# Attention values on 64 columns: neighbouring key tiles in two column halves, gathered in phases

## The reference, cut to what matters

```python
s_c = einsum(qg, k_cmp);  p_c = masked_softmax(s_c, ...)      # 63 compressed blocks
o_c = einsum(p_c, v_cmp)
imp = einsum(p_c, overlap); idx = top_k(imp + forced, 8)      # 8 of 16 blocks of 64 keys
o_s = einsum(softmax over the selected keys, v_s)             # selected branch
o_w = einsum(softmax over the last 512 keys, v_w)             # window branch
o = g[0] * o_c + g[1] * o_s + g[2] * o_w
```

## Time and profile before

| | us |
|---|---|
| median of three runs | 3420.3 |
| the profiled execution | 3416.0 |
| its span in the trace | 3414.2 |
| attention, first value matmul to last output | about 615 |
| TensorE busy in the span | 3256.0 (95%) |
| VectorE busy | 1531.2 (45%) |
| ScalarE busy | 1229.9 (36%) |
| GpSimd busy | 289.7 (8%) |

### The profile page before, as it was taken

The page is one execution under the profiler, slowest core; times in us unless marked ns, Lnnn a source line. Parts: engine busy times, 40 slices in busy tenths (PEclk is TensorE's granted clock), DMA queues, the critical chain, the costliest instruction groups (busy, mean ns, idle before and its releaser), DMA issues.

```text
span 3414.2 us, 40195 instructions
## 1 busy us (share of the span) xinstructions
PE 3256.0 (95%) x15510; PEld 2674.1 (78%) x15510; DVE 1531.2 (45%) x2409; ACT 1229.9 (36%) x1919; POOL 289.7 (8%) x503
## 2 busy tenths in 40 slices
PE   7999987899999999999999999999978999999997
PEld 5888876788888887888888778667766788888886
DVE  6552456655553344543543542575545322323233
ACT  3641146666666123321321231375513321212121
POOL 0110013333323100000000000110000000000000
PEclk9999989999999999999999999999988999999999
DMA  3222310000000511111111131000101111111111
GB/s 131 81 77 72 117 62 1 1 1 1 1 1 1 186 60 43 49 49 49 49 49 44 49 122 50 25 1 24 40 19 50 62 50 49 49 49 44 48 50 68
DMA packets 48110, 168.35 MB, mean 49 GB/s; under 512 B 6784, under 2 KB 7936, under 8 KB 47600
## 3 DMA queue, kind: packets, MB, share of 16 engines
q1 hardware_dynamic: 37008, 126.49, 11.9%
q0 software_dynamic: 10976, 40.15, 3.3%
HBM read 144.07 MB, written 16.78 MB: 47 GB/s over the span
## 4 chain that ended last, share of the span: by engine, by line
PE 90%; DVE 5%; ACT 3%; issue 1%; DMA 0%; POOL 0%; SPq 0%; DVEq 0%; ACTq 0%
PE PS L223 66%; PE PS L802 6%; PE PS L243 2%; PE PS L793 2%; PE PS L1467 2%; PE PS L778 2%; PE PS L1443 2%; PE PS L777 2%; PE PS L1456 1%; PE PS L820 1%; PE PS L812 1%; DVE SST L1807 0%; PE PS L297 0%; DVE SST L1803 0%; ACT QS L573 0%
## 5 line engine op out<-in xcount | busy, mean ns | idle before, releaser
L201 DVE TENSOR_TENSOR WLO<-RAW,WHI 128x1024 fp32r<-128x1024 f32 x220 | 269.4, 1224 | 1020.5 <-ACT WHI L196 1020.1
L196 ACT CAST WHI<-RAW 128x1024 fp32r<-128x1024 f32 x220 | 231.4, 1052 | 1368.0 <-PE PS L223 1348.5
L223 PE MATMUL PS<-HLO,WHI 128*128 128x512 f32 x2176 | 671.1, 390 | 0.0
L223 PEld LDWEIGHTS PS<-HLO,WHI 128*128 128x128 f32 x2176 | 409.0, 188 | 85.5
L223 PE MATMUL PS<-X_HI,WHI 128*128 128x512 f32 x1520 | 470.5, 391 | 4.5 <-DVE W L318 2.2
L223 PE MATMUL PS<-X_HI,WLO 128*128 128x512 f32 x1520 | 468.0, 389 | 0.0
L223 PEld LDWEIGHTS PS<-X_HI,WHI 128*128 128x128 f32 x1520 | 284.2, 188 | 66.8 <-DVE W L318 2.7
L223 PEld LDWEIGHTS PS<-X_HI,WLO 128*128 128x128 f32 x1520 | 285.5, 188 | 59.5
L223 PE MATMUL PS<-HID_HI,WHI 128*128 128x512 f32 x864 | 267.0, 390 | 5.0 <-DVE HID_LO L1187 5.0
L223 PE MATMUL PS<-HID_HI,WLO 128*128 128x512 f32 x864 | 266.5, 390 | 0.0
L223 PE MATMUL PS<-HID_LO,WHI 128*128 128x512 f32 x864 | 266.5, 390 | 0.0
(11 more groups left out here) (308 smaller groups left out, 4772.0 us busy)
## 6 DMA issues: line engine op xcount, KB each, us to landing
RAW<-in_w SPq DMA_DIRECT2D x220, 512.0 KB, 3.6
X<-in_x SPq DMA_DIRECT2D x8, 512.0 KB, 8.0
Q<-QN POOLq DMA_DIRECT2D x32, 128.0 KB, 2.7
merged<-W POOLq DMA_DIRECT2D x8, 512.0 KB, 3.3
gate<-W POOLq DMA_DIRECT2D x8, 512.0 KB, 2.9
W<-gate POOLq DMA_DIRECT2D x8, 512.0 KB, 4.0
W<-merged POOLq DMA_DIRECT2D x8, 512.0 KB, 4.7
X<-in_x POOLq DMA_DIRECT2D x8, 512.0 KB, 10.9
```

The lines of the kernel that those rows point to most:

```text
L196: nc.scalar.copy(WHI[:, slot, :], RAW[:, slot, :]).then_inc(w_hi, 1)
L201: nc.vector.tensor_tensor(WLO[:, slot, :], RAW[:, slot, :], WHI[:, slot, :].bitcast(F32), ALU.subtract).then_inc(w_lo, 1)
L223: last = nc.tensor.matmul(o[:, half], w[:, slot, cols], x(k)[:, half], start=(k == 0 and w is WHI and x is hi), stop=(k == kcs - 1 and w i ...
```

## The change

The value matmuls take only the 64 columns of V of the pair's own group. The first tile of a chunk writes partitions 0 to 63 of `O_PS`, the second, and the compressed branch, partitions 64 to 127; the output's start partition places each in one column half of the array. The two halves are two partial sums: a new `dve_out_sum` copies the first from PSUM into `O_SUM` and adds the second, and then frees `O_PS`. `act_out_hi` and `dve_out_lo` read `O_SUM`, and a new semaphore `o_lo` stands where `o_free` stood at the end. The uses are gathered: a pair's chunks form one batch (up to four chunks) or two (the first has half of them, rounded up), and all matmuls of a batch stand together in TensorE's queue. The last batch of a pair is used in the next pair's iteration, behind the transposes of its first batch; the odd head's scores stand behind that. `PT` has eight buffers. `act_out_hi` stands behind copy 2 (or the last) instead of copy 0. `O_SUM` lies where `POOL_W` lay.

```diff
--- before.py
+++ after.py
@@ -133,6 +133,7 @@
     QK_W = fix("QK_W", [4])
     QS_W = fix("QS_W", [1])
     GATE = fix("GATE", [QT, N_GATE])
+    POOL_W_AT = at
     POOL_W = fix("POOL_W", [N_POOL, P])
     POOL_INV = fix("POOL_INV", [N_POOL, 16])
     POOL_SC = fix("POOL_SC", [N_POOL])
@@ -674,7 +675,8 @@
     MSEL = [sb(f"MSEL{i}", [T], X_AT + 8 * KB + 4 * KB * i) for i in range(2)]
     P_LONG = [sb(f"P_LONG{i}", [T + 5 * P], H_AT + 6656 * i) for i in range(4)]
     P_SHORT = [sb(f"P_SHORT{i}", [T], H_AT + 4 * KB * i) for i in range(6)]
-    PT = [sb(f"PT{i}", [4, P], W_AT + 12 * KB + 2 * KB * i) for i in range(4)]
+    PT = [sb(f"PT{i}", [4, P], (W_AT + 12 * KB if i < 4 else R + 24 * KB) + 2 * KB * i) for i in range(8)]
+    O_SUM = [sb(f"O_SUM{i}", [2, P], POOL_W_AT + KB * i) for i in range(2)]
     O_HI = sb("O_HI", [HPG, T], R, F32R)
     EC = sb("EC", [HPG, HEAD], W_AT)
     PCG = sb("PCG", [HPG, HEAD], W_AT + 2 * KB)
@@ -688,9 +690,9 @@
     T_PS = [PS[:, 2 * T + 512 * i:2 * T + 512 * i + 512] for i in range(2)]
     O_PS = [PS[:, 3 * T + 512 * i:3 * T + 512 * i + 2 * P] for i in range(2)]
     C0_PS = PS[:, 3 * T + 512:4 * T]
-    s_done, shifted, exp_done, inv_done, p_done, t_done, pt_copied, pv_done, o_hi, o_free = (
+    s_done, shifted, exp_done, inv_done, p_done, t_done, pt_copied, pv_done, o_hi, o_free, o_lo = (
         sem(n) for n in ("s_done", "shifted", "exp_done", "inv_done", "p_done", "t_done", "pt_copied", "pv_done",
-                         "o_hi", "o_free"))
+                         "o_hi", "o_free", "o_lo"))
     c_mm, c_shift, c_exp, c_gated = (sem(n) for n in ("c_mm", "c_shift", "c_exp", "c_gated"))
 
     def tiles_of(qt):
@@ -793,15 +795,27 @@
                 last = nc.tensor.transpose(T_PS[c % 2][:, P * (2 * x + e):P * (2 * x + e) + P], src, IDENT[:, :])
         last.then_inc(t_done, 1)
 
-    def pe_use(pe, m, i):
-
-        chunk = chunks_of(qt_of(m))[i]
-        pe.wait_ge(pt_copied, turned_at[m] + i + 1)
-        u = used_at[m] + i
-        for x, (branch, kt) in enumerate(chunk):
-            last = nc.tensor.matmul(O_PS[m % 2], (VS, VW)[branch][:, kt, :], PT[u % 4][:, 2 * x:2 * x + 2, :],
-                                    start=False, stop=(u + 1 == used_at[m + 1] and x == len(chunk) - 1))
-        last.then_inc(pv_done, 1)
+    def batches_of(m):
+
+        n = len(chunks_of(qt_of(m)))
+        cut = n if n <= 4 else (n + 1) // 2
+        return [range(0, cut)] + ([range(cut, n)] if cut < n else [])
+
+    def pe_use(pe, m, batch):
+
+        g = half_of(m // PAIRS % 2)
+        if batch[0] == 0:
+            pe_cmp_values(pe, m)
+        for i in batch:
+            chunk = chunks_of(qt_of(m))[i]
+            pe.wait_ge(pt_copied, turned_at[m] + i + 1)
+            u = used_at[m] + i
+            for x, (branch, kt) in enumerate(chunk):
+                last = nc.tensor.matmul(O_PS[m % 2][half_of(x), :], (VS, VW)[branch][:, kt, g],
+                                        PT[u % 8][:, 2 * x:2 * x + 2, :], start=(i == 0 and x == 0),
+                                        stop=(u + 1 == used_at[m + 1] or (x == 1 and u + 2 == used_at[m + 1]
+                                              and len(chunks_of(qt_of(m))[-1]) == 1)))
+            last.then_inc(pv_done, 1)
 
     def pe_cmp_values(pe, m):
         s, pair = m // PAIRS, m % PAIRS
@@ -809,7 +823,8 @@
         if m >= 2:
             pe.wait_ge(o_free, m - 1)
         x = 2 * (pair % 2)
-        nc.tensor.matmul(O_PS[m % 2], VCZ[pair // 2][:, :], PCT[s % 2][:, x:x + 2, :], start=True, stop=False)
+        nc.tensor.matmul(O_PS[m % 2][half_of(1), :], VCZ[pair // 2][:, half_of(s % 2)], PCT[s % 2][:, x:x + 2, :],
+                         start=True, stop=False)
 
     def pe_cmp_scores(pe, s):
         qt, g = s // 2, s % 2
@@ -840,26 +855,27 @@
         pe_scores(pe, 2)
         pe_scores(pe, 3)
         for m in range(PAIRS_ALL):
-            s, ahead, chunks = m // PAIRS, ahead_of(m), len(chunks_of(qt_of(m)))
+            s, ahead = m // PAIRS, ahead_of(m)
             if ahead:
                 pe_scores(pe, 2 * ahead)
             if m % PAIRS == 0 and s + 1 < SEGS:
                 pe_cmp_scores(pe, s + 1)
             if m % PAIRS == 2 and s + 1 < SEGS:
                 pe_cmp_turn(pe, s + 1)
-            pe_turn(pe, m, 0)
-            if chunks > 1:
-                pe_turn(pe, m, 1)
-            pe_cmp_values(pe, m)
-            pe_use(pe, m, 0)
+            b = batches_of(m)
+            for i in b[0]:
+                pe_turn(pe, m, i)
+            if m:
+                pe_use(pe, m - 1, batches_of(m - 1)[-1])
             if ahead and not waits_for_all(m):
                 pe_scores(pe, 2 * ahead + 1)
-            for i in range(1, chunks):
-                if i + 1 < chunks:
-                    pe_turn(pe, m, i + 1)
-                pe_use(pe, m, i)
+            if len(b) > 1:
+                for i in b[1]:
+                    pe_turn(pe, m, i)
+                pe_use(pe, m, b[0])
             if ahead and waits_for_all(m):
                 pe_scores(pe, 2 * ahead + 1)
+        pe_use(pe, PAIRS_ALL - 1, batches_of(PAIRS_ALL - 1)[-1])
 
     def act_exp(act, n, branch):
         p = probs_of(n, branch)[:, 0:width_of(n, branch)]
@@ -870,9 +886,9 @@
     def act_copy(act, m, i):
         c, u, n = turned_at[m] + i, used_at[m] + i, 2 * len(chunks_of(qt_of(m))[i])
         act.wait_ge(t_done, c + 1)
-        if u >= 4:
-            act.wait_ge(pv_done, u - 3)
-        nc.scalar.copy(PT[u % 4][:, 0:n, :], T_PS[c % 2][:, 0:P * n].rearrange("p (x q) -> p x q", q=P))\
+        if u >= 8:
+            act.wait_ge(pv_done, u - 7)
+        nc.scalar.copy(PT[u % 8][:, 0:n, :], T_PS[c % 2][:, 0:P * n].rearrange("p (x q) -> p x q", q=P))\
             .then_inc(pt_copied, 1)
 
     def act_cmp_scores(act, s):
@@ -894,12 +910,12 @@
         qt = qt_of(m)
         return tile[half_of(m // PAIRS % 2), heads_of(m), P * qt:P * qt + P]
 
-    def o_ps_of(m):
-        return O_PS[m % 2][half_of(m // PAIRS % 2), :].rearrange("p (x q) -> p x q", q=P)
+    def o_sum_of(m):
+        return O_SUM[m % 2][half_of(m // PAIRS % 2), :, :]
 
     def act_out_hi(act, m):
-        act.wait_ge(pv_done, used_at[m + 1])
-        nc.scalar.copy(out_of(O_HI, m), o_ps_of(m)).then_inc(o_hi, 1)
+        act.wait_ge(o_free, m + 1)
+        nc.scalar.copy(out_of(O_HI, m), o_sum_of(m)).then_inc(o_hi, 1)
 
     def act_attention(act):
         for i, s_ in enumerate(g1_out):
@@ -917,7 +933,7 @@
                 act_cmp_copy(act, s + 1)
             for i in range(chunks):
                 act_copy(act, m, i)
-                if i == 0 and m:
+                if i == min(2, chunks - 1) and m:
                     act_out_hi(act, m - 1)
                 for x, after in enumerate(exp_after(m, chunks)):
                     if ahead and i == after:
@@ -1011,10 +1027,18 @@
         dve_select(dve, 0)
         dve_select_mask(dve, 0)
 
+    def dve_out_sum(dve, m):
+        dve.wait_ge(pv_done, used_at[m + 1])
+        if m >= 2:
+            dve.wait_ge(o_lo, m - 1)
+        parts = [O_PS[m % 2][half_of(i), :].rearrange("p (x q) -> p x q", q=P) for i in range(2)]
+        seq(dve, nc.vector.tensor_copy(o_sum_of(m), parts[0]))
+        nc.vector.tensor_tensor(o_sum_of(m), parts[1], o_sum_of(m), ALU.add).then_inc(o_free, 1)
+
     def dve_out_lo(dve, m):
         dve.wait_ge(o_hi, m + 1)
-        nc.vector.tensor_tensor(out_of(HLO, m), o_ps_of(m), out_of(O_HI, m).bitcast(F32), ALU.subtract)\
-            .then_inc(o_free, 1)
+        nc.vector.tensor_tensor(out_of(HLO, m), o_sum_of(m), out_of(O_HI, m).bitcast(F32), ALU.subtract)\
+            .then_inc(o_lo, 1)
 
     def dve_attention(dve):
         for n in range(4):
@@ -1039,12 +1063,16 @@
                     dve_select(dve, s + 1)
                     dve_select_mask(dve, s + 1)
             if m:
-                dve_out_lo(dve, m - 1)
+                dve_out_sum(dve, m - 1)
             if ahead:
                 dve_shift(dve, 2 * ahead + 1, 0)
                 dve_shift(dve, 2 * ahead + 1, 1)
                 dve_inverse(dve, 2 * ahead)
+            if m:
+                dve_out_lo(dve, m - 1)
+            if ahead:
                 dve_inverse(dve, 2 * ahead + 1)
+        dve_out_sum(dve, PAIRS_ALL - 1)
         dve_out_lo(dve, PAIRS_ALL - 1)
 
 
@@ -1056,7 +1084,7 @@
     x_back = [sem(f"x_back{k}") for k in range(KC)]
 
     def pool_merge(pool):
-        pool.wait_ge(o_free, PAIRS_ALL)
+        pool.wait_ge(o_lo, PAIRS_ALL)
         for i in range(2):
             pool.wait_ge(mp_out[i], 64)
         for i, s_ in enumerate(g1_out):
@@ -2094,7 +2122,7 @@
             pe_unit(pe, U_G1 + t, hi_of(0), h_lo)
             pe_compress(pe, t)
         pe_attention(pe)
-        pe.wait_ge(o_free, PAIRS_ALL)
+        pe.wait_ge(o_lo, PAIRS_ALL)
         for t in range(KC):
             pe_unit(pe, U_BR + t, lambda k: O_HI[:, k, :], h_lo)
         for t in range(KC):
```

## The result

The changed kernel takes 3451.3 us (median; 3442.7 to 3451.9), the kernel before 3419.6 us beside it (3417.1 to 3422.1): a ratio of 1.0086, interval 1.0070 to 1.0102. It is 0.9% slower. The forecast was 3408, its range 3368 to 3450. The profiled execution has a span of 3449.3 us against 3414.2.

A forecast was written before the change was run, and what follows sets the result against it. TensorE bounds the kernel, 97 to 99% busy from `qt` 4 on. Stage terms -3 -5 -4 +1 -9 -1 -3 +11 and +1 at the end give -12 us: 3404 profiled, 3408 median; range 3368 to 3450.

The forecast's parts named there:

- TensorE's saving: 592 value matmuls in 96 phases: overlapping column halves save 107.6 us; 192 mode switches at 0.12 cost 23.
- the 85 us of work: What TensorE was to lose over the attention: the overlap's 107.6 us less 23 for mode switches.
- The rival of no overlap: Value matmuls: column halves don't run side by side; +66 us, 23 of switches and stretched loops, 3510; 12%.
- The walk at `qt` 7: One steady pair followed through the queues: 13.6 us instead of 12.13, TensorE idle before chunks 5 and 6; stage +11.
- s + 4.34: `qt` 7 pair: chunk 5's transposes start 4.34 us after s, the start of the odd head's scores.
- the rival at 30%: From `qt` 5 on, TensorE's idle stretches lower its clock, adding 15 to 30 us: 3425 to 3440; chance 30%.
- the single wait of 1.3 us: Counted against a falling clock: TensorE's clock in the kernel before held through single waits of 1.3 us.
- the step that failed: Stages `qt` 0 to 2, where uses come one pair later than their copies: -3, -5 and -4 us.
- the 51 us of wait: TensorE's wait before value matmuls' weight loads, for copies of turned probabilities: 51.0 us, to largely go.
- the edit that I let be covered: ScalarE's `act_out_hi` waits for `o_free`, odd exp queued behind; at `qt` 0 and 1, already in the stage numbers.
- 4 x 0.6 us: `qt` 0 and 1: VectorE's chain for the segment stays and gets this much longer; clean pairs shorten by 1 to 2.
- the loop through E3: `qt` 7: odd head's scores, shift, first exp (E3), copy 3, chunk 5, last use, next scores: 13.6 us a pair.

The follow-up runs named there:

- e10: e4 with the odd head's two exps each one copy later (behind copies 3 and 4): 3371.9 us, ratio 0.9863.
- e1: The changed kernel with value matmuls at the full 128 columns, its queue orders and VectorE's two instructions a pair kept: 3514.6 us, ratio 1.0277.
- e8: e4 with value matmuls at the full 128 columns, so its queue orders without the column halves: 3448.9 us, ratio 1.0086.
- e2: The changed kernel with TensorE's order of the kernel before, each chunk used at once in two halves, no batches: 3447.0 us, ratio 1.0082.
- e7: The changed kernel with four unneeded matmuls before chunk 5's transposes in `qt` 7's pairs, filling TensorE's idle time: 3447.0 us, ratio 1.0079.
- e4: The changed kernel with odd scores before the use, sum behind odd shifts and an inverse, `act_out_hi` behind copies and exps, `dve_out_lo` last: 3388.7 us, ratio 0.9905.
- e5: The changed kernel with only the VectorE and ScalarE moves of e4, TensorE's order as changed: 3419.1 us, ratio 0.9997.
- e6: The changed kernel with `act_out_hi` alone moved, behind the pair's last copy and exps: 3465.0 us, ratio 1.0130.
- e11: The changed kernel with the odd head's two exps each one copy later (behind copies 3 and 4): 3403.8 us, ratio 0.9957.
- e9: The changed kernel with three unneeded matmuls before the first transposes of pairs at `qt` 0 to 2, filling TensorE's idle time: 3446.5 us, ratio 1.0079.

## Why the prediction was wrong, step by step

**TensorE's saving: right.** A phase of 5 matmuls takes 1029.11 - 1027.67 = 1.44 us in e10, the way out of the mode included (predicted 1.3 + 0.1), and one of 9 takes 1033.11 - 1030.81 = 2.30 (2.17 + 0.1): the fuller half's 3 or 5 matmuls of 0.434, and 0.14. The way in shows where 2 transposes take 1030.81 - 1030.44 = 0.37 instead of 0.22. So a phase costs 0.15 + 0.14 = 0.29 us of switching where the sum had 0.24, 5 us in 96 phases. Of the 85 us of work that the prediction takes off TensorE, 60 to 63 reach the end time with the orders held fixed (e1, e8). The rival of no overlap is out. The prediction counts (n + 1) x 0.217 for a phase of n; the rows, e2's phases of two among them, fit a phase as long as its fuller half, which is the same for odd n and 0.217 less for even n. The Trainium skill's rule that a weight load overlaps running matmuls only when its row group differs ("TensorE: Matmul & The Clock Gate", Part 3) would have given that rival; the two matmuls that start at 1095.84 and the 0.217 us for each matmul of a phase speak against it for column halves.

**The walk at `qt` 7: right, but for the clock.** Chunk 5's transposes were predicted at s + 4.34 and came at s + 4.27 (1094.18 - 1089.91), chunk 6's at 5.63 to 5.86 and 5.56. The stage was predicted at 97 + 11 = 108; e7, with the clock at 1.00, has 108.1. The same walk held at `qt` 4 (-9 predicted, -6.8 measured).

**The clock: what the rival at 30% describes happened, for less than its price.** It asked for the lower level in the use behind the idle stretches. The trace shows 0.63 there, 0.91 over the stage, 0.97 at `qt` 5 and 6. The measured 3451.3 us lies outside its 3425 to 3440, and would lie inside without the loss at `qt` 0 to 2. Its 15 to 30 us were too much: at `qt` 7 it is up to 9 us, by the executions profiled. At `qt` 5 and `qt` 6, which miss by some 6 us each, a clock of 0.97 over about 100 us makes about 3 (an estimate from the windows); the other half I can't place. In my forecast I held the single wait of 1.3 us for evidence that the clock stays up; the idle stretches walked were longer, and in two parts.

**`qt` 0 to 2: the step that failed.** I took -12 us and got +12.5. Two terms were mis-sized. First, I let the 51 us of wait before the value matmuls turn into time saved. They are waits of the weight loads; the value matmuls themselves wait 22.8 us for copies in the whole attention (18.0 and 4.8), and only 11.5 of it lie in these stages. What TensorE waits for next was left out. With every order mended (e10) the stages take 165.1 us, against 164.2 before and 152.2 predicted, and TensorE waits there for the copy of the compressed branch's `PCT`, which stands behind VectorE's work for the segment, and 10.2 us for VectorE's shifts, in front of scores. Two lines of before, then one of e10, each over its `qt` 0 to 2:

```profile
PE PS L793 <- ACT PCT L886: 12.8, 4, 3.8
PE PS L802 <- ACT PT L875: 11.5, 13, 1.6
...
PE PS L795 <- ACT PCT L902: 16.6, 4, 4.8
```

That is 13 of the 24.5 us. The halves bring nothing here: e4 has 165.2 us, and e8, the same orders at full width, 163.8. Two causes are seen and not told apart. VectorE has two instructions a pair more (35.5 us busy at `qt` 0, before 30.7). And at `qt` 0 the granted clock is lower with the halves: 0.55 in e4 and 0.63 in e10, against 0.79 in e8, where the compressed scores take 1.95 us instead of 3.62 and the stage 43.2 instead of 47.3. The sum had no term for the clock here. Why it is lower there stays open, and not every stretch at the lower level costs time: e4 and e10 have the same code at `qt` 0 and both take 47.3 to 47.4 us. Second, the edit that I let be covered, `act_out_hi` waiting for the sum: at `qt` 1, pair 2 of a segment, it stands in front of the even head's exps while the sum stands behind the whole selection on VectorE.

```profile
562.55 0.42 DVE L1035 COPY O_SUM<-PS 64x256 f32<-64x256 f32 x1
563.47 0.40 ACT L918 CAST O_HI<-O_SUM 64x256 fp32r<-64x256 f32 x1 [5.67 <-DVE O_SUM L1036]
...
565.75 0.56 ACT L902 COPY PCT<-PS 128x512 f32<-128x512 f32 x1
566.37 1.11 PE L795 MATMUL PS<-IDENT,P_SHORT 128*128 128x128 f32 x4 [4.79 <-ACT PCT L902]
```

ScalarE waits 5.67 us, and TensorE 4.79 behind it; in e5 TensorE waits 3.58 at the same place. With the sum and `O_HI` moved (e5) the three stages fall from 176.7 to 165.6. That is the other 11. I had counted 4 x 0.6 us for it. Not all of it is that wait: `O_HI` moved alone (e6) leaves the stages at 176.5, and 6.0 of e5's 11.1 lie at `qt` 0, where its clock is 0.75 for 0.64. How the 11 divide between the two moves and the clock isn't shown.

**In sum**, measured less predicted: +24.5 at `qt` 0 to 2, -5 at `qt` 3, +2 at `qt` 4, +11 at `qt` 5 and 6, +9 at `qt` 7, and 6 behind the attention that no part of the change explains. The forecast got the new bound at `qt` 7 right (the loop through E3) and what it costs at the upper clock level; it mis-sized the stages that TensorE never bound, and had no term for the lower clock.

## What to carry to other kernels

A gain in one engine's work is worth what the in-order queues of the others let through: here 60 us of saving were there all along, and the place of the odd head's two exps in ScalarE's queue decided between 0.9% slower and 0.4% faster. When a use is gathered or delayed, follow each queue past its end: whatever stands behind the instruction that consumes it (here the shifts behind the sum) is now tied to it, so put consumers that nobody waits for last. And where the engine made faster was idle already, count nothing, and look whether its clock falls: at `qt` 0 the halves came with a stage 4.1 us longer.

## What the runs showed of the hardware

- Two 64-column matmuls on different column halves start in the same 0.01 us, and in a phase a float32 matmul of 256 columns costs 0.217 us instead of 0.434.
- Going from full-width transposes to the half-width phase and back costs about 0.29 us together (0.15 and 0.14). That is small in a phase of nine and about two thirds of the 0.43 us that a phase of two saves (e2).
- In the changed kernel at `qt` 7 the clock fell behind idle stretches of 1.98 and 0.64 us with 0.66 us of transposes between them (0.63 in the 4 us after), but not in the stage's first two pairs, which have the same stretches and stayed at 1.00; the stage stayed at 1.00 with one stretch of 1.54 us in each pair (e11). The same code showed 0.91 over `qt` 7 in one profile and 0.98 in another (e9), so a time worked out from either level alone is off by up to 9 us here.
- At `qt` 0 sixteen matmuls of 64 columns in a row took 3.62 us at a clock of 0.50 (the changed kernel) and 1.95 us at 1.00 (e5, e8, e9). ScalarE's copy behind them waited 2.45 us in the changed kernel and 0.64 in e5.
